# Two half slots per gather and column tiles of TensorE for the weighted sum in the expert stages

## The reference

```python
def peer_rows(xr, w_query, sub_keys, expert_u, expert_v):
    q = (xr @ w_query).reshape(n, PEER_HEADS, 2, PEER_DHALF)
    s = jnp.einsum('nhcd,ckd->nhck', q, sub_keys)
    # top 16 of both halves, their 256 sums, top 16 of these: top_s, eidx
    gate = jax.nn.softmax(top_s, axis=-1)
    u = expert_u[eidx]
    h = jax.nn.gelu(jnp.einsum('nhkd,nd->nhk', u, xr), approximate=False)
    out = jnp.einsum('nhk,nhkd->nd', gate * h, expert_v[eidx])
```

## Time and profile before

| | us |
|---|---|
| median of three runs | 3503.53 (3502.59 to 3512.5) |
| the profiled execution | 3500.28 |
| its span | 3498.5 |
| TensorE busy | 2615.5 (75%) |
| VectorE busy | 1768.4 (51%) |
| ScalarE busy | 659.7 (19%) |
| GpSimd busy | 946.1 (27%) |
| moved by DMA | 959.04 MB, mean 274 GB/s |
| chain that ended last: DMA of `pair_ring` | 18% |
| the same: TensorE at L1436 | 6% |

### The profile page before, as it was taken

One profiled execution on the slowest core, in us unless ns is written; L12 is line 12 of the kernel. 1 busy time (PEld: TensorE's weight loads), 2 busy tenths in 40 slices (PEclk: granted clock), 3 DMA queues, 4 the chain that ended last, 5 costly groups with the idle time before them and its releaser, 6 DMA issues. The chain is left out here.

```text
span 3498.5 us, 32692 instructions
## 1 busy us (share of the span) xinstructions
PE 2615.5 (75%) x11853; PEld 1419.4 (41%) x11853; DVE 1768.4 (51%) x4015; ACT 659.7 (19%) x1800; POOL 946.1 (27%) x929
## 2 busy tenths in 40 slices
PE   7949494866977777777777794887877777777776
PEld 3427383753842322232222343666733222322222
DVE  1133534322558657855555204432778567755555
ACT  0022121220121211122112103311111211121112
POOL 0013130310044433444434000000144434443332
PEclk9979696987999999999999895988999999999999
DMA  5220204023599999999999412523699999999997
GB/s 176 86 107 2 73 1 100 1 44 131 164 391 420 420 420 420 403 420 420 420 420 420 160 66 120 223 103 101 242 416 412 420 420 420 407 420 420 420 420 319
DMA packets 193198, 959.04 MB, mean 274 GB/s; under 512 B 33232, under 2 KB 67200, under 8 KB 94736
## 3 DMA queue, kind: packets, MB, share of 16 engines
q0 software_dynamic: 114784, 821.12, 56.9%
q1 hardware_dynamic: 78256, 135.84, 11.6%
HBM read 938.81 MB, written 18.12 MB: 274 GB/s over the span
## 5 line engine op out<-in xcount | busy, mean ns | idle before, releaser
L1436 PE MATMUL pacc<-pair_ring,diag 128*128 128x512 f32 x3072 | 1439.5, 615 | 489.0 <-ACT diag L1415 488.9
L1289 POOL DMA_INDIRECT pair_ring<-in_peer_uv,expert x768 | 800.9, 1043 | 1679.4 <-PE pacc L1436 1089.6
L1386 DVE CUSTOM_DVE_ANT_0 pair_ring<-pair_ring,x_tok 128x1024 f32<-128x1024 f32 x768 | 939.5, 1225 | 622.5 <-DMA pair_ring<-in_peer_uv,expert 619.5
L1436 PEld LDWEIGHTS pacc<-pair_ring,diag 128*128 128x128 f32 x3072 | 571.2, 195 | 1356.0 <-issue 1344.6
L1410 ACT ACTIVATE acts<-dots 128x2 f32<-128x2 f32 x384 | 78.1, 203 | 1384.3 <-DVE dots L1386 1384.0
L1415 ACT ACTIVATE diag<-constants_sb,mix 128x128 f32<-128x128 f32 x768 | 266.2, 393 | 145.0 <-DVE mix L1392 143.2
L1130 PE MATMUL pbank<-peer_xT,wq 128*128 128x128 f32 (+1 forms) x1024 | 178.3, 340 | 14.0 <-DMA wq<-in_peer_w_query 14.0
L1130 PEld LDWEIGHTS pbank<-peer_xT,wq 128*128 128x128 f32 x1024 | 162.9, 201 | 29.5 <-DMA wq<-in_peer_w_query 15.3
L275 PE MATMUL acc<-w_ring,mixed 128*128 128x512 f32 x288 | 125.8, 599 | 10.0 <-issue 9.1
L1487 PE MATMUL aacc<-aw_ring,at_xT 128*128 128x512 f32 x288 | 126.4, 601 | 6.2 <-DMA aw_ring<-in_w_kv 5.6
L1392 DVE TENSOR_TENSOR mix<-gate,acts 128x2 f32<-128x2 f32 x384 | 59.6, 155 | 68.0 <-ACT acts L1410 68.0
(11 more groups left out here) (372 smaller groups left out, 2639.1 us busy)
## 6 DMA issues: line engine op xcount, KB each, us to landing
wq<-in_peer_w_query SPq DMA_DIRECT2D x32, 1024.0 KB, 5.9
cache_k<-in_cache_k SPq DMA_DIRECT2D x8, 2048.0 KB, 12.2
cache_v<-in_cache_v SPq DMA_DIRECT2D x8, 2048.0 KB, 8.7
w_ring<-in_rwkv_w_rkv SPq DMA_DIRECT2D x24, 512.0 KB, 3.3
pair_ring<-in_peer_uv,expert POOLq DMA_INDIRECT x768, 18.4
aw_ring<-in_w_kv SPq DMA_DIRECT2D x16, 512.0 KB, 8.6
pn_w_rwkv<-in_rwkv_w_out SPq DMA_DIRECT2D x8, 512.0 KB, 7.1
aw_ring<-in_diff_w_q SPq DMA_DIRECT2D x8, 512.0 KB, 3.2
```

The source lines that it names most:

```text
L1289: pool.indirect_dma_start(ring[:, g % RING, :], None, io["peer_uv"], bass.IndirectOffsetOnAxis(ap=expert[:, t, s:s + 1], axis=0)).then_inc ...
L1386: dve.tensor_tensor_reduce(ring[:, g % RING, 0:D], ring[:, g % RING, 0:D], x[:, t, :], 1.0, 0.0, ALU.mult, ALU.add, dots[:, t % 2, s:s + 1 ...
L1436: mm = pe.matmul(acc[:, half, :], diag[:, g % DIAGS, :], ring[:, g % RING, D + half * HALF:D + (half + 1) * HALF], start=(s == 0), stop=(s ...
```

## The change

A gather now holds two half slots. With 64 tokens `w` in a half `j` of the tile, gather `(q, j)` brings for partition `w` the row of slot `q` of token `64 j + w`, and for partition `64 + w` the row of slot `64 + q` of the same token. It is still 128 rows of 8 KB, and there are still 128 gathers for a tile. The weights of a gather become two 64x64 diagonals, one above the other (128x64), and the matmul of gather `(q, j)` writes PSUM partitions `64 j` to `64 j + 63` only, in column tile `j` of TensorE. The matmuls of the two gathers of a turn alternate between the column tiles, half by half.

For this the tokens, the expert numbers and the gates have to lie in the new order. SyncE copies the tokens of each tile in four DMAs from `x_tok` to `rows` (1 MB). Expert numbers and gates go through HBM: out in one DMA, back in two. For the expert numbers of tile 0 GpSimd does this itself; all others are SyncE's. `gate` has one buffer, so `choose` waits until the old gates have gone out. The two-place ring of `others` lies in the last two places of the gather ring, and the gather of slot 8 waits until its products are made. The exponential of the next tile's gates comes at slot 88 for 96, its sums at 94 for 102.

The core of the diff:

```diff
+GROUPS = 2
+FOLD = P // GROUPS
+TURNS = SLOTS // GROUPS
+    put("fold_ident", row % FOLD == np.arange(FOLD)[None, :])
 ...
-    RING, DIAGS, BATCH = 10, 6, 2
-    TURNS = SLOTS // BATCH
+    RING, DIAGS = 10, 3
+    BORROWED = RING - 2
-    EXP_AT, SUM_AT, ROOT_AT, SCALE_AT = 96, 102, 112, 118
+    EXP_AT, SUM_AT, ROOT_AT, SCALE_AT = 88, 94, 112, 118
 ...
-        diag = sb("diag", [P, DIAGS, P])
+        diag = sb("diag", [P, DIAGS, GROUPS, FOLD])
-        others = KeyScores(core, io, ctx, xT, scores, layer, (1, 2), 2)
+        others = KeyScores(core, io, ctx, xT, scores, layer, (1, 2), 2, wq=ring[:, BORROWED:].rearrange("p r (k n) -> p r k n", k=KD))
 ...
+        def turn_out(eng, t, src, scratch, out):
+            eng.dma_start(scratch[t], src).then_inc(*out.by(16))
+        def turn_in(eng, t, dst, scratch, out, landed_in):
+            eng.wait_ge(*out)
+            for s in range(GROUPS):
+                eng.dma_start(dst[s * FOLD:(s + 1) * FOLD], scratch[t].rearrange("(j w) (s q) -> s w j q", w=FOLD, q=TURNS)[s]).then_inc(*landed_in.by(16))
 ...
             def _(sp):
+                def spread_rows(t):
+                    for s in range(GROUPS):
+                        for j in range(GROUPS):
+                            sp.dma_start(rows[s * FOLD:(s + 1) * FOLD, t % 2, j, :], core.x_tok[j * FOLD:(j + 1) * FOLD, t, :]).then_inc(*rows_in.by(16))
+                spread_rows(0)
                 others.loads(sp)
 ...
+                sp.wait_ge(*soft_done.at(1))
+                turn_out(sp, 0, gate[:], core.turn_gate, gate_out)
+                turn_in(sp, 0, row_gate[:, 0], core.turn_gate, gate_out.at(16), gate_in)
+                for t in range(1, TILES):
+                    if t == 1:
+                        sp.wait_ge(*scored.at(8))
+                    else:
+                        sp.wait_ge(*dot_done.at((t - 1) * SLOTS))
+                    spread_rows(t)
+                    sp.wait_ge(*chosen.at(t + 1))
+                    turn_out(sp, t, expert[:, t, :], core.turn_at, at_out)
+                    turn_in(sp, t, row_at[:, t], core.turn_at, at_out.at(16 * t), at_in)
+                    sp.wait_ge(*soft_done.at(t + 1))
+                    turn_out(sp, t, gate[:], core.turn_gate, gate_out)
+                    turn_in(sp, t, row_gate[:, t % 2], core.turn_gate, gate_out.at(16 * (t + 1)), gate_in)
 ...
             def _(pool):
+                pool.wait_ge(*chosen.at(1))
+                turn_out(pool, 0, expert[:, 0, :], core.turn_at, first_out)
+                turn_in(pool, 0, row_at[:, 0], core.turn_at, first_out.at(16), first_in)
+                pool.wait_ge(*first_in.at(16 * GROUPS))
                 for t in range(TILES):
-                    pool.wait_ge(*chosen.at(t + 1))
+                    if t > 0:
+                        pool.wait_ge(*at_in.at(16 * GROUPS * t))
 ...
+                        elif g == BORROWED:
+                            pool.wait_ge(*others.q_psum.at(HC))
-                                                bass.IndirectOffsetOnAxis(ap=expert[:, t, s:s + 1], axis=0)).then_inc(*row_in[g % RING].by(16))
+                                                bass.IndirectOffsetOnAxis(ap=row_at[:, t, j, q:q + 1], axis=0)).then_inc(*row_in[g % RING].by(16))
 ...
                     if t > 0:
                         dve.wait_ge(*scored.at(4 * t))
+                        dve.wait_ge(*gate_out.at(16 * t))
 ...
+                    dve.wait_ge(*rows_in.at(16 * GROUPS * GROUPS * (t + 1)))
 ...
+                            if q == 0:
+                                dve.wait_ge(*gate_in.at(16 * GROUPS * (t + 1)))
 ...
+                            act.activation(diag[:, n % DIAGS, j, :], core.const("fold_ident"), ACT.Copy,
+                                           scale=mix[:, t % 2, q, j:j + 1]).then_inc(*diag_done.by())
 ...
                         for half in range(2):
-                            mm = pe.matmul(acc[:, half, :], diag[:, g % DIAGS, :], ring[:, g % RING, D + half * HALF:D + (half + 1) * HALF],
-                                           start=(s == 0), stop=(s == SLOTS - 1))
-                        mm.then_inc(*row_used.by())
+                            for j in range(GROUPS):
+                                g = n * GROUPS + j
+                                if half == 0:
+                                    pe.wait_ge(*landed(g))
+                                    pe.wait_ge(*diag_done.at(g + 1))
+                                mm = pe.matmul(acc[j * FOLD:(j + 1) * FOLD, half, :], diag[:, n % DIAGS, j, :],
+                                               ring[:, g % RING, D + half * HALF:D + (half + 1) * HALF],
+                                               start=(q == 0), stop=(q == TURNS - 1), tile_position=(0, j * FOLD))
+                                if half:
+                                    mm.then_inc(*row_used.by())
```

More of the change, by code:

```diff
@@ L1094, with __init__ @@
     PAIR = 2 * P
[L1096 removed]
+    def __init__(self, core, io, ctx, xT, scores, layer, tiles, ring, wq=None, qT=None):
         def sb(name, shape, dt=F32):
@@ L1249, in peer_experts @@
         expert = sb("expert", [P, TILES, SLOTS], U32)
-        gate, dots, acts, mix = (sb(n, [P, 2, SLOTS]) for n in ("gate", "dots", "acts", "mix"))
+        gate = sb("gate", [P, SLOTS])
+        row_at, row_gate = sb("row_at", [P, TILES, GROUPS, TURNS], U32), sb("row_gate", [P, 2, GROUPS, TURNS])
+        dots, acts, mix = (sb(n, [P, 2, TURNS, GROUPS]) for n in ("dots", "acts", "mix"))
+        rows = sb("rows", [P, 2, GROUPS, D])
         best, best_at = sb("best", [P, HC, PTOP]), sb("best_at", [P, HC, PTOP], U32)
```

60 lines of the change are left out of this document (30 added, 30 removed).

## The result

Four runs of the changed kernel have a median of 3546.94 us (3544.04 to 3549.2), beside 3508.02 us (3502.59 to 3513.53) for four of the kernel before: 1.011 times as long, with a 95% interval of 1.0088 to 1.0132. It is 38.9 us slower. The forecast of 3525 us was 21.5 us above the median of before that was known then, and is 17.0 us above this one. It named the direction rightly and 3547 lies inside its range of 3506 to 3550, but the change costs about twice what was put. The profiled execution took 3545.58 us against 3500.28, so 45.3 us are to be found.

A forecast was written before the change was run, and what follows sets the result against it. DMA bounds the kernel at 420 GB/s without slack; TensorE's work counts only where DMA runs dry. Per layer 8.7 + 0 + 2.5 + 2.6 - 1.2 - 1.8 = 10.8 us, both 21.6, so 3525 us against 3503.5; range 3506 to 3550.

The forecast's parts named there:

- Start of the stream: Start of each layer's gathers: token copies and the trips of numbers and gates delay the twelfth gather 8.7 us (bounds 3, 12).
- the return of the gates: Tile 0, softmax to first `mix`: gates back at 996 (bounds 990.7 and 999), each small piece waiting for one 8 KB row.
- Bytes added to the stream: Each layer: tile 1's tokens 0, tile 2's tokens 2.5 us, small pieces of numbers and gates 2.6 us.
- The first gather at +6 (bounds 5 to 8): Layer start: expert numbers go out and back before GpSimd's first gather, moving it from 960.7 to about 966.7.
- Alone this costs nothing: Layer start: the later first gather is free, since ten gathers end near 995 and the eleventh waits for TensorE anyway.
- The softmax shifted by 2 us (bounds 1.5 to 4): Layer start: token copies ahead of key and query loads move the softmax's end from 983.42 to 985.4.
- Small pieces and dips: Each layer: pieces of numbers and gates cost 2.6 us; three dips behind `choose` give back 1.2 us.
- Tail: End of each layer: the last turn falls from 3.67 to about 1.9 us; with the narrower diagonal this saves 1.8 us.
- The quick trip (B): Small pieces pass the gathers, gates back at 990.7, a layer costs 2.2 us: 3508; chance 0.19.
- the column tiles don't run together (C): TensorE's turn stays 3.67 us, the tail saves nothing, restarts come later, some 3 us more a layer: 3531; chance 0.23.
- weight loads lie bare (D): Uncovered weight loads make TensorE's turn 4.96 us against 4.99 of DMA; with 0.2 us of waits a turn, 3600; chance 0.05.
- E: Whole kernel faster by over 0.3% from dips, holes and tail; under 12 us to gain before any cost; chance 0.03.

The follow-up runs named there:

- full width: The changed kernel with its column tiles undone, each matmul over both diagonals at once (128 columns): 3553.37 us, 1.0138.
- the early copies: The changed kernel with a token buffer for all three tiles, all token copies issued between the query loads: 3545.14 us, 1.0126.
- The run with half the pieces: The changed kernel with tile 0's tokens copied behind the query loads and its gates brought back by one DMA instead of two: 3553.66 us, 1.0128.

## Why the prediction was wrong in its size, and what of it was right

**The steps that failed.** The sum put 10.8 us a layer, and 20.7 and 23.3 were measured. Two of its terms carry most of the difference. In "Start of the stream" (8.7 put, 13.7 and 13.3 measured) the step that failed is the return of the gates: it was priced at one 8 KB row of wait for each small piece, which put `mix` at 996.3, +89; it came at +94.7, about when the gathers in flight had landed. In "Bytes added to the stream" the step that failed is the tokens of tile 2, priced at their bytes, 2.5 us; they cost 6.5 and 6.6 us, since the copies between 64 partitions slow the stream. Small pieces, dips and tail together add the remaining 0.9 us in layer 0 and 3.8 us in layer 1.

**The bound and the stream: right.** Each steady window shows 420 GB/s and 40 gathers, and neither 1.5 us less of TensorE in a turn (2.14 for 3.67) nor the same 1.5 us given back (full width) moved it. The turn at the upper level was put at 1.9 us.

**The start: the mechanism was right, the term was 5 us too small** (8.7 put, 13.7 and 13.3 measured). Three steps of it failed, and not all of them cost time.
- *The first gather at +6 (bounds 5 to 8).* It came 9.0 us late. Out took the 2.2 us of a small load, but back took 6.8: it ran beside the 1 MB query loads of `others`, and I had priced it on idle queues.
- *"Alone this costs nothing."* The eleventh gather does wait for TensorE, but TensorE waits for the gates, and these are back only about when the gathers in flight have landed. My own upper bound for the gates was the end of the gathers plus the rest after it, 999; it lacked the 3 us by which the gathers themselves end later. 999 + 3 is 1002, less 907 is +95; measured is +94.7. So the bound held as a rule while the value taken inside it, 996, rested on one 8 KB row of wait for each piece. In all kernels with the trip `mix` stands between +91.6 and +96 (layer 1 of the early copies aside), whether the gates left at +76 or at +85.
- *The softmax shifted by 2 us (bounds 1.5 to 4).* It shifted by 8: the keys came 5 us later, the products waited behind the slow copies and ended 4 us late, and the scores after them took 4 us more, for a reason that I did not look for. This miss was the largest and costs nothing: taking it away gave nothing back.

Removing the gates' trip brought the twelfth gather 10.2 and 10.9 us forward, the trip itself 6.8 and 7.0 of it, so that trip is most of the term; with all of tile 0 in the old order the term is 0 in layer 1. Without the trip 3.6 and 2.4 us of the term are left, in a kernel whose softmax still ends 4.7 and 3.7 us later than before. The late first gather by itself was worth 1.8 and 0.6 us in the kernel that sent no numbers. How a small transfer gets its turn beside a full stream stays open: one row for each piece is too little (the way out takes 6.6 to 7.4 us where 2.7 us of waiting on top of 2.2 were put). "All gathers first" fits the way back but not the way out, which is done 5 to 9 us before the gathers have landed when the gates leave at +76 to +78, and takes as long in the steady stream, which doesn't drain. The run with half the pieces did not settle it.

**Tokens of tile 1 at nothing: right**, as long as the hole is there. Without the gates' trip they cost their 6.5 us.

**Tokens of tile 2 at 2.5 us (bounds 1.2 to 5): the second mis-sized term.** They cost 6.5, beyond the upper bound. My upper bound doubled the bytes for a copy within SBUF; what makes it slow is the shape, 64 partitions at a time, and with 128 the 4.0 us on top go away.

**Small pieces and dips.** 2.6 − 1.2 = 1.4 us was put, 2.1 and 3.5 remain. (The way out goes in pieces of 512 B, not 256, so by the prediction's own working the 2.6 should have been 2.9; and the hole of layer 1 is 5.1 us, not 5.2.) Behind the costly steps of `choose` the stream now loses 3.8 us in layer 0 and 6.9 in layer 1, by the working of the earlier trace rows over all windows of a layer, where 3.5 and 4.8 were lost before. So the −1.2 turned into +0.3 and +2.1, and 1.8 and 1.4 us are left for the pieces, less than the 2.6.

**Tail.** The time from the last diagonal to the PSUM copy fell from 4.25 us to 2.67 in layer 0, −1.6 where −1.8 was put. In layer 1 it is 4.17:

```profile
3525.60 0.59 ACT L1467 ACTIVATE diag<-constants_sb,mix 128x64 f32<-128x64 f32 x2 [0.23 <-DVE mix L1445]
...
3526.09 3.64 PE L1491 MATMUL pacc<-pair_ring,diag 128*64 128x512 f32 x8 [2.84 <-ACT diag L1467]
...
3529.77 1.01 ACT L1474 COPY scores<-pacc 128x1024 f32<-128x1024 f32 x1 [3.58 <-PE pacc L1491]
```

The last turn fell near the lower level (granted clock 0.57 over its 3.64 us) and takes 3.64 us, as long as the wide one before. I had said that a slower turn would be hidden; in the tail nothing hides it.

**The rivals.** The quick trip (B) needed the gates before 992; they came at 1003. That the column tiles don't run together (C), and that weight loads lie bare (D), both fall with turns of 2.14 us and with the pair of kernels that changed only the width. E was not met by the change, though 8.5 of the 12 us that it named as a limit could be had in another way.

## What to carry to other kernels

Where a full stream sets the time, do not price a small transfer by its own size. Here the way out took 6.3 to 7.4 us for 64 KB and the way back lasted about until the stream ahead of it had landed. Keep it off the path that restarts the stream: send it before the stream begins or let nothing depend on it. Copy within SBUF over all 128 partitions; a half-partition copy takes the DMA engines about 6.5 us a megabyte beside a full stream where 2.5 were due. And before work is taken off an engine, ask where it is waited for: 1.5 us of 5 saved in each turn gave some 2 us a layer, while two more places in the ring gave 4.5 and 6.1, part of it not theirs.

## What the runs showed of the hardware

Three things I had not expected. A transfer of 64 KB in 128 pieces takes 2.2 us to HBM on quiet queues and 6.3 to 7.4 beside the stream (6.4 in the changed kernel at a place where nothing waits for it):

```profile
1163.11 0.33 SPq L1285 DMA_DIRECT2D turn_at<-expert  x1
...
1169.48 1.27 SPq L1291 DMA_DIRECT2D row_at<-turn_at  x2
```

Back, in half rows, it takes 2.8 to 3.5 us when the gathers have landed and 6.8 to 10.5 when they have not.

A DMA share of 1.0 is no proof of full rate: during the half-partition copies the share stays at 0.98 to 1.06 with 270 to 278 GB/s moved.

And with TensorE busy for less of the time, its granted clock went down to 0.77 in the steady window (over the whole execution 0.82 too in the kernel before with column tiles, and 0.917 in the changed one at full width), so that the same eight records took 2.14 us in one turn and 3.67 in the next. Less work on TensorE brought a lower clock with it, and in one of two tails that took back nearly all that the narrower work had gained.
